# Eight experts written out as straight code for each engine, one compare per width, a hinted branch at each body's end, and the row transposes among the down products

## The reference

```python
D_MODEL = 1024; N_EXPERTS = 8; TOP_K = 2; D_FF_E = 1408

def moe_swiglu(h, w_router, b_router, w1, w3, w2):
    logits = h @ w_router + b_router
    top_v, top_i = lax.top_k(logits, TOP_K)
    gates = jax.nn.softmax(top_v, axis=-1)
    comb = jnp.sum(jax.nn.one_hot(top_i, N_EXPERTS) * gates[..., None], axis=-2)
    y = jnp.zeros_like(h)
    for e in range(N_EXPERTS):
        y = y + comb[..., e:e + 1] * ((silu(h @ w1[e]) * (h @ w3[e])) @ w2[e])
    return y
```

## Time and profile before

| | |
|---|---|
| timed runs | 1823.43, 1825.82, 1828.92 us; median 1825.82 |
| the profiled execution | span 1826.2 us |
| PE busy | 1479.6 us, 81% of the span |
| DVE, ACT, POOL busy | 602.4, 480.2, 397.8 us |
| DMA | 286.02 MB, mean 157 GB/s |
| mean granted TensorE clock | 0.914 of full speed |

### The profile page before, as it was taken

One profiled execution on the slowest core, in us unless ns is written; L12 is line 12 of the kernel. 1 busy time (PEld: TensorE's weight loads), 2 busy tenths in 40 slices (PEclk: granted clock), 3 DMA queues, 4 the chain that ended last, 5 costly groups with the idle time before them and its releaser, 6 DMA issues.

```text
span 1826.2 us, 27269 instructions
## 1 busy us (share of the span) xinstructions
PE 1479.6 (81%) x11320; PEld 1411.8 (77%) x11321; DVE 602.4 (33%) x815; ACT 480.2 (26%) x662; POOL 397.8 (22%) x288
## 2 busy tenths in 40 slices
PE   5776877789999999989588859879796919949792
PEld 4555876679999999979577649869796919949692
DVE  6667697623112011146965320101101000000115
ACT  6677312422221122223133221111111100011114
POOL 1102560534434343434524020000000000000004
PEclk9998898899999999989899979889898959979896
DMA  9999121024333322322210469686685833637554
GB/s 321 300 337 316 48 91 46 28 70 120 93 87 98 105 93 56 96 93 70 69 47 6 164 218 306 209 295 210 241 269 183 300 109 110 216 104 234 173 171 163
DMA packets 249862, 286.02 MB, mean 157 GB/s; under 512 B 7589, under 2 KB 241719, under 8 KB 249686
## 3 DMA queue, kind: packets, MB, share of 16 engines
q1 hardware_dynamic: 244886, 272.17, 45.9%
q0 software_dynamic: 3632, 11.08, 1.8%
q10 hardware_dynamic: 1200, 0.56, 0.1%
HBM read 266.45 MB, written 18.05 MB: 156 GB/s over the span
## 4 chain that ended last, share of the span: by engine, by line
PE 66%; DVE 15%; issue 9%; DMA 5%; SPq 2%; ACT 1%; POOL 1%; POOLq 0%; ACTq 0%; DVEq 0%
PE PP L747 28%; PE PP L1006 20%; PE PP L1019 10%; DVE work L1477 7%; DMA mem<-in_w_ada 4%; PE PP L760 2%; DVE stat L1573 1%; PE PP L988 1%; PE PP L792 1%; PE PP L721 1%; PE PP L732 1%; SPq L424 1%; PE PP L1028 1%; DVE stat L1406 1%; DVE mem L1419 1%
## 5 line engine op out<-in xcount | busy, mean ns | idle before, releaser
L747 PE MATMUL PP<-hT_r,mem_r 128*128 128x260 f32 x2624 | 428.5, 284 | 4.6 <-DVE xT L1431 3.2
L1006 PE MATMUL PP<-big,mem 128*128 128x128 f32 (+4 forms) x2816 | 362.4, 293 | 49.5 <-issue 49.2
L1006 PEld LDWEIGHTS PP<-big,mem 128*128 128x128 f32 x2816 | 360.6, 195 | 52.1 <-issue 49.6
L604 POOL TENSOR_TENSOR mem_r<-mem,mem_r 128x1024 fp32r<-128x1024 f32 (+1 forms) x108 | 279.0, 2597 | 407.5 <-ACT mem_r L1132 406.9
L747 PEld LDWEIGHTS PP<-hT_r,mem_r 128*128 128x128 f32 x2624 | 362.4, 188 | 6.4 <-issue 2.5
L747 PE MATMUL PP<-mem_r 128*128 128x260 f32 x1312 | 263.8, 283 | 0.0
L747 PEld LDWEIGHTS PP<-mem_r 128*128 128x128 f32 x1312 | 201.7, 188 | 0.0
L1019 PE MATMUL PP<-big,mem 128*128 128x128 f32 (+4 forms) x1408 | 184.2, 288 | 0.0
L1019 PEld LDWEIGHTS PP<-big,mem 128*128 128x128 f32 x1408 | 178.1, 191 | 0.0
L703 POOL DMA_INDIRECT mem<-y_by_expert,place x10 | 9.6, 956 | 720.7 <-DMA y_by_expert<-work 717.9
L1666 DVE TENSOR_TENSOR big<-PP,big 128x256 f32<-128x256 f32 x88 | 37.4, 425 | 381.3 <-ACT big L1313 381.3
(11 more groups left out here) (239 smaller groups left out, 1155.1 us busy)
## 6 DMA issues: line engine op xcount, KB each, us to landing
mem<-in_w_moe SPq DMA_DIRECT2D x48, 1536.0 KB, 9.8
mem<-in_w_ada SPq DMA_DIRECT2D x48, 1024.0 KB, 11.2
mem<-in_w_moe SPq DMA_DIRECT2D x32, 1408.0 KB, 8.8
mem<-in_w_dense SPq DMA_DIRECT2D x20, 1024.0 KB, 5.6
mem<-in_w_in SPq DMA_DIRECT2D x16, 1024.0 KB, 5.5
mem<-in_w_moe SPq DMA_DIRECT2D x16, 1024.0 KB, 7.0
mem<-in_w_dense SPq DMA_DIRECT2D x16, 704.0 KB, 4.9
mem<-in_w_out SPq DMA_DIRECT2D x8, 1024.0 KB, 5.1
```

The source lines that it names most:

```text
L604: pool.tensor_tensor(r_(raw), raw, read_(hi), ALU.subtract).then_inc(w_lo, 1)
L747: mm = pe.matmul(PP[q][:, h, 0:HT], r_(w[:, k, :]), r_(x[:, k, HT * h:HT * h + HT]), start=(i == 0 and w is wh and x is hi), stop=(i == le ...
L1006: mm = pe.matmul(PP[w][:, f % 2, 0:n], expert_slot(2 * c + w, KD, m)[:, k, P * (f % 3):P * (f % 3) + P], hn[:, k, 0:n], start=(k == 0), st ...
```

## The change

The loops over the experts become straight code on PE, ACT, DVE and SP. PE loads all eight counts and their maximum into registers before the first expert. Each expert has five bodies in place of ten (`WIDTHS`). An expert starts with one compare per width: the count either fits and the body follows at once, or PE jumps to the next compare. Each body but the widest marks a place after its fourth down product (`mark_branch_hint_location`) and ends in a branch to the next expert that carries this hint. The row transposes of expert e+1 stand after the down products q = 3 and q = 5 of expert e, one tile each; the transposes of the last output block (j = 7) stand after the next expert's second up block. SP loads the next expert's rows after the second chunk of an expert, and stores the last expert's rows there too. The code for large counts becomes a second pass over all experts in windows of 256 rows behind one If on the largest count; it does not run with these inputs. POOL waits for one semaphore that SP raises after this If.

```diff
-WIDTHS = [128, 136, 144, 152, 160, 176, 192, 208, 224, NW]
+WINDOWS = (T + NW - 1) // NW
+ROOM = PICKS + WINDOWS * NW
+WIDTHS = [144, 160, 176, 208, NW]
...
@@ sync: the experts
-            with sp.Fori(0, NE - 1) as e:
-                rest_of_rows(e)
-                row = first_of(sp, e + 1)
...
-                first_rows(row)
-                for j in range(PER_E):
...
-                    sp.wait_ge(which, n)
-                    j += EXPERT_RING
-                    eload(j, expert_chunk(e, j) if j < PER_E else expert_chunk(e + 1, j - PER_E))
-                rows_out(e)
...
+            for e in range(NE):
+                before_row = row
                 for j in range(PER_E):
+                    if e + 1 < NE or j + EXPERT_RING < PER_E:
+                        sp.wait_ge(*used(e, j))
+                        eload(j, expert_chunk(e, j + EXPERT_RING) if j + EXPERT_RING < PER_E else
+                              expert_chunk(e + 1, j + EXPERT_RING - PER_E))
+                    if j == 1 and e:
+                        rows_out(e - 1, last_row)
+                    if j == 1 and e + 1 < NE:
+                        row = first_of(sp, e + 1)
+                        sp.wait_ge(R["in_tr"], 2 * e + 2)
+                        rows_in(row)
+                last_row = before_row
+            rows_out(NE - 1, last_row)
+
+            with sp.If(tokens_of(sp, NE) > NW):
...
+            sp.wait_ge(R["y_out"], 32 * NE)
+            sp.sem_inc(R["y_all"], 1)
...
@@ gpsimd
-            pool.wait_ge(R["y_out"], 16 * NE * NT + 16)
-            pool.wait_ge(R["y_done"], NE * KD)
+            pool.wait_ge(R["y_all"], 1)
...
@@ tensor
+            def expert(e, n, c):
 
                 for f in range(ET):
...
+                            mm = pe.matmul(PP[w][:, f % 2, 0:n], raw[:, w, k, :], hn[:, k, 0:n], start=(k == 0), stop=(k == KD - 1))
                     mm.then_inc(R["f_done"], 1)
...
+                    if f == 1 and e:
+                        y_tr(e - 1, KD - 1)
                 for q in range(KD):
...
+                    mm.then_inc(R["y_done"], 1)
+                    if q:
+                        y_tr(e, q - 1)
+                    if q in (3, 5) and e + 1 < NE:
+                        rows_tr(e + 1, (q - 3) // 2)
+                    if q == 3 and n < NW:
+                        over = pe.mark_branch_hint_location()
+                if n < NW:
+                    pe.br_lt(c, T + 1, on_true=f"expert_over{e}", on_false=f"expert_over{e}").branch_hint(over)
+                else:
+                    pe.br(f"expert_over{e}")
...
+            def by_width(e, c, widths):
+
+                n, here = widths[0], f"expert{e}_of_{widths[0]}"
                 if len(widths) == 1:
...
+                pe.br_lt(c, n + 1, on_true=here, on_false=f"expert{e}_over_{n}")
+                with nc.body(here, valid_engines=[pe.engine]):
+                    expert(e, n, c)
+                with nc.body(f"expert{e}_over_{n}", valid_engines=[pe.engine]):
+                    by_width(e, c, widths[1:])
...
-            with pe.Fori(0, NE) as e:
-                c = tokens_of(pe, e)
-                with pe.If(c <= NW):
-                    narrow_rows(e)
-                    narrow_by_width(e, c, WIDTHS)
-                with pe.Else():
-                    wide(e)
-
-            pe.wait_ge(R["f_free"], ET * NE + 2)
+            counts = [tokens_of(pe, e) for e in range(NE + 1)]
+            for t in range(2):
+                rows_tr(0, t)
+            for e in range(NE):
+                by_width(e, counts[e], WIDTHS)
+                nc.switch_bb(f"expert_over{e}")
+            y_tr(NE - 1, KD - 1)
+
+            with pe.If(counts[NE] > NW):
...
@@ scalar, after the last Silu of the last expert
+                if e == NE - 1:
+                    act.dma_start(gf, A["g_final"].rearrange("(a n) -> a n", a=1).to_broadcast([P, D])).then_inc(gf_in, 16)
...
@@ vector, routing
-            link(dve.tensor_reduce(countf[:], PP[0][:, 1, 0:NT * NE].rearrange("p (t e) -> p e t", t=NT), AX.X, ALU.add))
+            link(dve.tensor_reduce(countf[:, 0:NE], PP[0][:, 1, 0:NT * NE].rearrange("p (t e) -> p e t", t=NT), AX.X, ALU.add))
+            link(dve.tensor_reduce(countf[:, NE:NE + 1], countf[:, 0:NE], AX.X, ALU.max))
```

More of the change, by code:

```diff
@@ L472, in used, with rows_in @@
                 return R["y_done"], KD * e + 2 * (j - 8) + 2
-            def first_rows(row):
+            def rows_in(row):
                 for t in range(2):
                     sp.dma_start(stage[:, t, :], Hd[bass.ds(row + P * t, P), :]).then_inc(Rin[t], 16)
[L479 to L507, removed]
+            def rows_out(e, row):
+                for t in range(2):
+                    sp.wait_ge(R["yt_ev"], 4 * e + 3 + t)
+                    sp.dma_start(Yd[bass.ds(row + P * t, P), :], yrow[:, t, :]).then_inc(R["y_out"], 16)
@@ L529, in _ @@
[L529 to L534 removed]
+            rows_in(row)
+            for e in range(NE):
+                before_row = row
+                for j in range(PER_E):
+                    if e + 1 < NE or j + EXPERT_RING < PER_E:
[7 more added lines that the diff above has]
+                        sp.wait_ge(R["in_tr"], 2 * e + 2)
+                        rows_in(row)
+                last_row = before_row
@@ L1071, in narrow_by_width @@
-            def narrow_by_width(e, c, widths):
+                    if KD * e + q >= 2:
+                        pe.wait_ge(R["y_free"], KD * e + q - 1)
+                    for k in range(ET):
+                        if q == 0 and k in (0, ET - 1):
+                            pe.wait_ge(R["f_free"], ET * e + (ET - 1 if k == 0 else ET))
+                        mm = pe.matmul(PP[2][:, q % 2, 0:n], expert_slot(PER_E * e + 8 + q // 2, ET, 256)[:, k, P * (q % 2):P * (q % 2) + P],
+                                       Gn[:, k, 0:n], start=(k == 0), stop=(k == ET - 1))
@@ new lines, in _ @@
+            for e in range(NE):
+                for f in range(ET):
+                    dve.wait_ge(R["f_act"], ET * e + f + 1)
+                    dve.tensor_tensor(Gn[:, f, :], PP[1][:, f % 2, 0:NW], hactn[:, f % 2, :], ALU.mult).then_inc(R["f_free"], 1)
+                    if e and f == 1:
+                        y_rows(e - 1, 1)
+                if e + 1 < NE:
+                    rows_even(e + 1, 0)
+                if e:
+                    dve.wait_ge(R["y_out"], 32 * e)
+                y_rows(e, 0)
+                if e + 1 < NE:
+                    rows_even(e + 1, 1)
```

343 lines of the change are left out of this document (171 added, 172 removed).

## The result

| | before | after |
|---|---|---|
| median of the timed runs | 1827.01 us (1823.43 to 1828.92, 4 runs) | 1732.95 us (1731.22 to 1735.85, 4 runs) |
| span of the profiled execution | 1826.2 us | 1730.9 us |
| ratio | | 0.9491, 95% interval 0.9475 to 0.9506 |

A forecast was written before the change was run, and what follows sets the result against it. PE bounds the kernel, with 124.6 us idle put down to taken branches. From 1826.2 us, less 96.8 for the stage, plus 0.2 for routing and 2 at the end, came 1731.6, stated as 1731; range 1712 to 1760.

The forecast's parts named there:

- the stage: PE from its first row transposes to its last output transposes: 610.1 us against 706.9 before, a gain of 96.8.
- Products at 144 columns: Up products of an expert at 144 columns on PE: 16 groups of 2.70 us, 43.2 us.
- Row transposes: PE's transposes of seven experts' rows, now among products at full clock: 12.3 us.
- copies before the first expert: Copies of the first expert's transposed rows, now waited for whole before its products: about 0.9 us.
- The clock: Lower PE clock after the idle time left at two expert entries: 3 us.
- Forward jumps: Four unhinted jumps to the next compare on PE, 4.7 us each, less 2.4 hidden at two entries: 14.0 us idle.
- The bound of 24: Upper bound on idle time from the four unhinted forward jumps: 6.0 us each, nothing hidden, 24 us.
- Closing branches: Eight hinted branches ending the experts' bodies on PE: 1.0 us each, 8 in all, bounds 0 and 28.
- The first rival: The hint does nothing and closing branches wait for their code: 1749 to 1776 us, about 1760; chance 0.17.
- Straight code: Rival: PE's straight code can't be fetched as fast as it runs, 188 us on top, 1919; chance 0.04.
- hidden wait for weights: Rival: PE's 124.6 us of idle time isn't the branches' and stays, about 1833 us; chance 0.04.
- The end: SP's count load and branch before POOL's gather, beside the last store: 2 us more, bounds 0 and 5.

The follow-up runs named there:

- the shifted kernels: The changed kernel with 64, 128 or 192 do-nothing instructions ahead of the first expert on PE: 1736.63, 1741.81 and 1741.11 us.
- the two runs on the hint: The changed kernel with plain closing branches, no hint: 1757.54 us; the changed kernel with the hint behind the last down product, not the fourth: 1763.44 us.

## Why the prediction was right

**What bounds the stage.** The idle time was the price of taken branches: the change without its hint, the ten widths and the five widths each move it with the jumps, and the jumps' own times fill the gaps. From its first row transposes at 1076.77 to the last output transposes, 1685.60, the stage took 608.8 us; 610.1 was the sum.

**Its terms.** Products at 144 columns took 43.36 us for the up part, of which the last 0.17 lie under the next row (43.2 in the sum). Row transposes took 0.87 a tile as counted, copies before the first expert 0.83 (0.9). The clock cost about 2 in the sixth expert (13.27 + 50.80 against 16 x 3.87 = 61.9) and nothing in the seventh, 3 in the sum.

**Two terms were off, in opposite ways.** Forward jumps: four at 4.7, or 18.8 less 4.8 for queued products, were predicted. They took 7.62, 4.95, 4.94 and 4.78 us, 22.3 in all: three at about the price taken, one above the 6.0 that the dearest row of before gave, with a transfer of weights beside it. (The 4.2 each that I read for seven jumps before was an average over unlike ones: these seven compares took 3.89, 0.25, 5.20, 4.95, 4.92, 4.83 and 4.84 us.) The bound of 24 held. Closing branches: 8 us of idle time predicted, 1.0 each. Six delayed nothing. The fifth expert's took 3.76 us, of which the queued products hid 2.3, with the three jumps still to come; what the sixth's 0.36 adds can't be told from the 2.43 us behind it. The idle time came to 22.0, as 14.0 and 8 do, which is chance: the jumps were counted too cheap, the closings too dear. The reason I gave for the 8, that a jump may land where the next piece of code is not yet there, is what the shifted kernels show. The one term is not a price per branch at all, but one per place.

**The hint.** The first rival, at 0.17, is shown false by the two runs on the hint: without it the time is 1757.5, near the 1760 that I gave, and the closings take 3.3 to 5.5 us in place of 0.3. The Trainium skill's sentence that prefetch is purely sequential (Runtime: NRT & Kernel Launch, Instruction fetch mechanics) does not fit the hinted branches here, and the measurement decides. Its other half, that a taken branch to code not at hand waits for a fetch, agrees: each jump before the sixth expert has two packets of code beside it and takes 4.9 us or more, and the ways round the loop that took 1.3 us have none.

**The other rivals.** Straight code did keep up, with gaps inside a body only right behind a landing; and the idle time was no hidden wait for weights.

**The end.** The gather begins 2.0 us later, 2 in the sum. The terms differ: of the 3.83 us behind SP's branch 1.3 lie past the landing of the last store, and that store itself took 4.3 us in place of 3.24.

**What I did not see** is how the gain is made up. By the ratios to before, the shorter table alone gives 2.9%, the change with ten widths 2.7%, the change without hints 3.8%, all of it 5.1%. My sum charged the widths with 28 us and credited the change as a whole with the branches; the table's own share, which pays those 28 and 52 more, stands nowhere in it.

## What to carry to other kernels

Idle time that "issue" explains and that grows with the depth of an If/Else chain was code here, not data: count the taken branches whose target has not just run, before anything else. Here few wide variants beat many narrow ones as long as a failed compare jumped over a body, and variants reached from compares that stand together need one jump each. On PE a hint paid 12 us ahead of its branch and did nothing right ahead of it; on SP it gained nothing. A gain or loss of a few us at such a branch says little about the edit, since moving the code by 64 instructions does as much.

## What the runs showed that was not expected

- Before the sixth expert PE is idle for 19.54, 20.04 and 20.19 us in three kernels and for 15.12 to 15.13 in the three shifted ones, at the same weights. In the first three the closing ahead of the same three failed compares took 3.76, 5.52 and 5.01 us, in the shifted ones 0.31 to 0.32.
- Before an expert with a single far jump PE is idle for 2.27 to 9.85 us within one kernel, though the jumps themselves took 4.41 to 7.21: what comes on top is a closing that was not free.
- A gap of 2 us at a branch cost PE up to 1.74 us more in the next two up blocks (9.75 against 8.01) by the clock granted behind it, but not each time (8.08 behind 2.00 us in the same kernel).
- On SP a hint 30 us ahead of its branch gained nothing; on DVE, in the same kernel, the idle time behind the branch fell from 3.62 to 1.70 us. The count was loaded earlier there too, and what each of the two gave can't be told apart.
